# Hybrid decoder step: the third weight tile ahead of the gate sums, two modulation blocks strung through it

## What is computed

```
mod = silu(c) @ w_ada + b_ada -> shift, scale, gate
h   = rms_norm(x) * (1 + scale) + shift
z   = h @ w_in      # att q,k,v,gate | mLSTM q,k | v | o | gate | i,f logits | merge gates A, B
A   = attention: prompt causal over own and past blocks of 256; samples: the 3 best of 8 cached
      blocks of 256 keys by q . mean(k), from a paged cache of 128-row pages, plus themselves
B   = conv(4) + silu on q,k; mLSTM (4 heads, qk 128, v 256) with exponential input gate, sigmoid
      forget gate and running maximum; per-head norm; output gate
u   = sigmoid(ga) * ((A * silu(za)) @ w_att) + sigmoid(gm) * ((B * silu(zm)) @ w_mlstm)
y   = rms_norm(x + gate * (u @ w_out));   also new k, v, C, n, m and conv states
```

## Time and profile before

| | us |
|---|---|
| three runs, median (lowest to highest) | 761.38 (760.47 to 762.78) |
| the profiled execution | 761.64 |
| its span, first to last instruction | 759.9 |
| TensorE busy | 687.3 (90%) |
| TensorE weight loads busy | 617.6 (81%) |
| VectorE busy | 484.9 (64%) |
| GpSimd busy | 467.6 (62%) |
| ScalarE busy | 337.4 (44%) |

### The profile page before, as it was taken

The page is one execution under the profiler, slowest core; times in us unless marked ns, Lnnn a source line. Parts: engine busy times, 40 slices in busy tenths (PEclk is TensorE's granted clock), DMA queues, the critical chain, the costliest instruction groups (busy, mean ns, idle before and its releaser), DMA issues.

```text
span 759.9 us, 14941 instructions
## 1 busy us (share of the span) xinstructions
PE 687.3 (90%) x5066; PEld 617.6 (81%) x5066; DVE 484.9 (64%) x467; ACT 337.4 (44%) x760; POOL 467.6 (62%) x294
## 2 busy tenths in 40 slices
PE   2789999998989789966999999999899999999992
PEld 0565788786868768965999999999799998999992
DVE  1530479998998975867679479498766259333222
ACT  5533483836264335434436446342422224333554
POOL 4210167665676814886698878957495556666652
PEclk9989799999999989997999999999799999999997
DMA  8973868988898871267596588579247355832102
GB/s 318 329 251 128 261 183 239 283 233 273 241 278 263 234 238 28 63 195 209 152 276 202 165 257 245 167 217 268 56 111 221 97 169 154 264 95 83 56 0 113
DMA packets 156903, 144.70 MB, mean 190 GB/s; under 512 B 7547, under 2 KB 115152, under 8 KB 156852
## 3 DMA queue, kind: packets, MB, share of 16 engines
q1 hardware_dynamic: 142696, 136.10, 59.8%
q10 hardware_dynamic: 14164, 8.07, 3.4%
HBM read 135.10 MB, written 9.11 MB: 190 GB/s over the span
## 4 chain that ended last, share of the span: by engine, by line
PE 52%; issue 13%; POOL 12%; DVE 11%; DMA 4%; SPq 4%; ACT 3%; POOLq 0%; ACTq 0%; DVEq 0%
PE ps L539 40%; POOL sb_wL L1408 5%; POOL sb_arenaA L1450 3%; POOL sb_arenaA L1480 3%; DVE sb_arenaA L1866 3%; SPq L391 2%; SPq L392 2%; PE ps L571 1%; PE ps L766 1%; PE ps L805 1%; DVE sb_arenaB L1871 1%; DMA sb_arenaA<-in_w_ada 1%; DMA sb_arenaB<-in_x_sample 1%; PE ps L643 1%; DVE sb_arenaA L1728 1%
## 5 line engine op out<-in xcount | busy, mean ns | idle before, releaser
L1408 POOL TENSOR_TENSOR sb_wL<-sb_wraw,sb_wH 128x512 fp32r<-128x512 f32 (+1 forms) x176 | 232.5, 1338 | 188.7 <-ACT sb_wH L951 173.5
L539 PE MATMUL ps<-sb_hH,sb_wH 128*128 128x260 f32 x1152 | 242.0, 292 | 10.6 <-DVE sb_hL L1632 6.8
L539 PE MATMUL ps<-sb_hL,sb_wH 128*128 128x260 f32 x1152 | 235.6, 287 | 0.0
L539 PE MATMUL ps<-sb_hH,sb_wL 128*128 128x260 f32 x1152 | 235.6, 286 | 0.0
L539 PEld LDWEIGHTS ps<-sb_hH,sb_wH 128*128 128x128 f32 x1152 | 181.8, 193 | 22.4 <-issue 17.0
L951 ACT ACTIVATE sb_wH<-sb_wraw 128x512 fp32r<-128x512 f32 (+1 forms) x176 | 103.5, 612 | 189.3 <-PE ps L539 131.3
L539 PEld LDWEIGHTS ps<-sb_hL,sb_wH 128*128 128x128 f32 x1152 | 181.9, 193 | 0.0
L539 PEld LDWEIGHTS ps<-sb_hH,sb_wL 128*128 128x128 f32 x1152 | 181.3, 192 | 0.0
L1480 POOL TENSOR_TENSOR sb_arenaA<-sb_arenaA 128x2048 f32<-128x2048 f32 x32 | 115.9, 3628 | 8.1 <-DMA sb_arenaA<-in_cache_v 6.1
L1450 POOL TENSOR_TENSOR sb_arenaA<-sb_arenaA 128x2048 f32<-128x2048 f32 x12 | 60.9, 5079 | 30.3 <-DMA sb_arenaA<-in_cache_k 30.3
L1728 DVE TENSOR_REDUCE sb_arenaA<-sb_arenaA 128x2048 f32 (+1 forms) x32 | 72.8, 2285 | 3.3 <-DVE sb_arenaA L1724 2.5
(11 more groups left out here) (356 smaller groups left out, 951.4 us busy)
## 6 DMA issues: line engine op xcount, KB each, us to landing
sb_wraw<-in_w_in SPq DMA_DIRECT2D x64, 512.0 KB, 5.2
sb_arenaA<-in_cache_k SPq DMA_DIRECT2D x128, 256.0 KB, 3.1
sb_arenaA<-in_cache_v SPq DMA_DIRECT2D x128, 256.0 KB, 3.4
sb_arenaA<-in_w_ada SPq DMA_DIRECT2D x6, 2048.0 KB, 12.3
sb_arenaB<-in_state_C SPq DMA_DIRECT2D x8, 512.0 KB, 4.0
sb_wraw<-in_w_mlstm SPq DMA_DIRECT2D x8, 512.0 KB, 4.4
sb_wraw<-in_w_out SPq DMA_DIRECT2D x8, 512.0 KB, 3.9
sb_arenaB<-in_x_prompt SPq DMA_DIRECT2D x1, 2048.0 KB
```

The lines of the kernel that those rows point to most:

```text
L539: last = mm(ps[:, 2 * s + a, 0:HALF], w[:, s, k, :], x[:, k, a * HALF:(a + 1) * HALF], start=(k == 0 and w is wH and x is xH), stop=(k == ...
L1408: tt(wL[:, j % 2, part], wraw[:, j % 4, part], wH[:, j % 2, part].bitcast(F32), ALU.subtract)\
```

## The change

- **Start and pair 0, TensorE.** Block 2 moves ahead of tile 0 (bank 2 instead of 4), block 3 and both turns ahead of tile 1's first half. Half of the gate logits comes before tile 0's second half, the other half strung through it, one k behind each k of the tile (`beside`). Tile 2 moves from behind the first scores to ahead of the gate sums, and blocks 5 and 6 are strung through it: behind k = 0..3 two k of block 5 each, behind k = 4..7 two k of block 6 each (`late_blocks`). The turned gate rows go to bank 7 instead of 6.
- **ScalarE** copies block 2 out before the activations k = 4, 6, takes the convolution states after block 3, and copies blocks 5 and 6 out behind the keys (tile 1).
- **GpSimd** leaves out the product of key step 5 in the last pair; **VectorE** does it itself after the loop. The loop over pairs on GpSimd is one trip shorter, with the last pair written out.
- **VectorE** reduces value pair 4 of head 0 behind the convolutions of head 1 instead of ahead of them.

```
--- before.py
+++ after.py
@@ -35,6 +35,7 @@
 AH, DH = 8, 64
 AW = AH * DH
 PAIRS = AW // P
+LAST = PAIRS - 1
 MH, MQ, MV = 4, 128, 256
 PAGE, PAGES = 128, 16
 NBLK = 8
@@ -524,7 +525,7 @@
             mm = nc.tensor.matmul
             tr = nc.tensor.transpose
 
-            def ztile(j, n, xH, xL, ks=KT, part_ready=None, pages_of=None, parts=(0, 1)):
+            def ztile(j, n, xH, xL, ks=KT, part_ready=None, pages_of=None, parts=(0, 1), beside=None):
                 s = j % 2
                 for half in parts:
                     if half == 0:
@@ -538,6 +539,8 @@
                                 for a in range(2):
                                     last = mm(ps[:, 2 * s + a, 0:HALF], w[:, s, k, :], x[:, k, a * HALF:(a + 1) * HALF],
                                               start=(k == 0 and w is wH and x is xH), stop=(k == ks - 1 and w is wL))
+                        if beside:
+                            beside((k,))
                     if half == 0:
                         last.then_inc(z_half, 1)
                 if pages_of is not None:
@@ -564,13 +567,14 @@
             last.then_inc(t_x, 1)
             pe.wait_ge(c_T, 1)
 
-            def modulation(i, bank):
+            def modulation(i, bank, ks=range(KT)):
                 pe.wait_ge(ld_ada[i % 2], 16 * (i // 2 + 1))
-                for k in range(KT):
+                for k in ks:
                     g = k % 4
                     last = mm(ps[32 * g:32 * g + 32, bank, :], (hS if i == W_Q else cT)[:, k, :], ada[:, i % 2, k, :],
                               start=(k < 4), stop=(k >= 4))
-                last.then_inc(ada_used, 1)
+                if k == KT - 1:
+                    last.then_inc(ada_used, 1)
 
             def mod_turn(count, slot, bank, col):
 
@@ -606,29 +610,31 @@
             prompt_turn(range(4, KT))
 
             pe.wait_ge(v_col, 1)
+            pe.wait_ge(mod_rdy, 2)
+            modulation(2, 2)
             ztile(0, T_ATT, hH, hL, part_ready=h_lo, parts=(0,))
-            pe.wait_ge(xT_act, 3)
-            modulation(2, 4)
-            ztile(1, T_ATT + 1, hH, hL, parts=(0,))
             pe.wait_ge(xT_dve, 5)
+            modulation(3, 5)
             mod_turn(3, 0, 7, 0)
             pe.wait_ge(ld_st, 16)
             pe.wait_ge(xT_act, 4)
             for k in range(KT):
                 last = tr(ps[:, 6, 24 * k:24 * k + 24], stC[:, k * P:(k + 1) * P], ident[0:24, 0:24])
             last.then_inc(t_x, 1)
-            modulation(3, 5)
             mod_turn(4, 1, 7, 36)
-
-            def gate_logits():
-                pe.wait_ge(if_lo, 1)
-                pe.wait_ge(xT_dve, 5)
-                for k in range(KT):
+            ztile(1, T_ATT + 1, hH, hL, parts=(0,))
+
+            def gate_logits(ks):
+                for k in ks:
                     for x in (hH, hL):
                         for bank, cols in ((4, slice(0, T // 2)), (5, slice(T // 2, NT))):
                             last = mm(ps[0:4 * MH, bank, 0:cols.stop - cols.start], wif2[:, k, :], x[:, k, cols],
                                       start=(k == 0 and x is hH), stop=(k == KT - 1 and x is hL))
-                last.then_inc(gt_mm, 1)
+                if k == KT - 1:
+                    last.then_inc(gt_mm, 1)
+
+            pe.wait_ge(if_lo, 1)
+            gate_logits(range(KT // 2))
 
             def qk(e, t):
                 r = slice(DH * e, DH * e + DH)
@@ -669,12 +675,11 @@
                 if before:
                     ztile(0, n, hH, hL)
                 else:
-                    ztile(0, n, hH, hL, part_ready=h_lo, parts=(1,))
+                    ztile(0, n, hH, hL, part_ready=h_lo, parts=(1,), beside=gate_logits)
                 if before:
                     pe.wait_ge(pnorm, 2 * t)
                     ptrans(1)
                 else:
-                    gate_logits()
                     modulation(W_Q, 7)
                 ztile(1, n + 1, hH, hL, parts=(0, 1) if before else (1,))
                 if not before:
@@ -683,16 +688,18 @@
                     pe.wait_ge(st_ev, 1)
                     mm(ps[0:B, 6, :], groupsum[:, 0:B], modp[:, 0, :], start=True, stop=True).then_inc(q_mm, 1)
                     pe.wait_ge(gt_ev, 1)
-                    modulation(5, 5)
                     pe.wait_ge(consts, 3)
-                    pe.wait_ge(q_ev, 1)
                     for j in range(TT + 1):
                         tok = slice(j * P, min((j + 1) * P, NT))
-                        last = mm(ps[0:tok.stop - tok.start, 6, 8 * j:8 * j + 8], gT[:, tok], pairsum[:, :],
+                        last = mm(ps[0:tok.stop - tok.start, 7, 8 * j:8 * j + 8], gT[:, tok], pairsum[:, :],
                                   start=True, stop=True)
                     last.then_inc(g_mm, 1)
-                    modulation(6, 4)
-
+
+                    def late_blocks(ks):
+                        k, = ks
+                        modulation(5 + k // 4, 5 - k // 4, range(2 * (k % 4), 2 * (k % 4) + 2))
+
+                    ztile(2, n + 2, hH, hL, beside=late_blocks)
                     pe.wait_ge(g_dve, 3)
                     for j in range(TT):
                         last = mm(ps[:, 7, MH * j:MH * j + MH], upper[:, :], lf[:, j, :], start=True, stop=(j == 0))
@@ -700,6 +707,7 @@
                             last = mm(ps[:, 7, MH * j:MH * j + MH], ones[:, :], lf[:, i, :], start=False,
                                       stop=(i == j - 1))
                     last.then_inc(g_pe, 1)
+                    pe.wait_ge(q_ev, 1)
                     mod_turn(5, 1, 6, 0)
                     mod_turn(6, 0, 6, 36)
                     pe.wait_ge(q_lo, 1)
@@ -716,8 +724,9 @@
                     for j in range(TT):
                         last = tr(ps[0:MH, 7, j * P:(j + 1) * P], ec[:, j, :], ident[:, :])
                     last.then_inc(g_pe, 1)
-                ztile(2, n + 2, hH, hL)
-                if not before:
+                if before:
+                    ztile(2, n + 2, hH, hL)
+                else:
 
                     pe.wait_ge(g_dve, 5)
                     for j in range(TT):
@@ -1027,14 +1036,14 @@
             high(0, 0, 0)
             high(1, 1, 0)
             prompt_high(0)
+            ada_leave(2, 2, 1).then_inc(ada_ev, 1)
             turned_out(4)
             turned_out(6)
-            ada_leave(2, 4, 1).then_inc(ada_ev, 1)
-            act.wait_ge(t_x, KT + 4)
-            f(stT[:, :, :].rearrange("p k n -> p (k n)"), ps[:, 6, 0:192], ACT.Copy).then_inc(st_ev, 1)
             act.wait_ge(ld_small, 64)
             f(wif2[:, :, 0:2 * MH], wif[:, :, :], ACT.Copy).then_inc(if_hi, 1)
             ada_leave(3, 5, 2).then_inc(ada_ev, 1)
+            act.wait_ge(t_x, KT + 4)
+            f(stT[:, :, :].rearrange("p k n -> p (k n)"), ps[:, 6, 0:192], ACT.Copy).then_inc(st_ev, 1)
             prompt_high(1)
 
             def gate_rows():
@@ -1116,11 +1125,12 @@
                     gate_rows()
                     ada_leave(W_Q, 7, 3).then_inc(qp_ev, 1)
                     sample_queries()
-                    ada_leave(5, 5, 4).then_inc(ada_ev, 1)
                     gate_logs()
-                    ada_leave(6, 4, 4).then_inc(ada_ev, 1)
                 samples_kept(1, n + 1, t)
                 leave(1, n + 1, kT, ACT.Copy)
+                if not before:
+                    ada_leave(5, 5, 4).then_inc(ada_ev, 1)
+                    ada_leave(6, 4, 4).then_inc(ada_ev, 1)
                 copy_out(0, t, before)
                 high(3, n + 3, quad)
                 weights(0, t)
@@ -1450,9 +1460,9 @@
                 tt(four, four, qbc[:, s // 4:s // 4 + 1, :].broadcast_to([P, STEP_PAGES, AW]), ALU.mult)\
                     .then_inc(pool_mult, 1)
 
-            def attention(t, before):
+            def attention(t, first, last):
                 n = T_ATT + 4 * t
-                if not before:
+                if first:
                     low(2, n + 2)
                     query_low()
                     low(3, n + 3)
@@ -1462,11 +1472,13 @@
                 low(2, n + 6)
                 key_step(7, t)
                 low(3, n + 7)
-                key_step(5, t)
-
-            attention(0, False)
-            with pool.Fori(0, PAIRS - 1) as t:
-                attention(t + 1, True)
+                if not last:
+                    key_step(5, t)
+
+            attention(0, True, False)
+            with pool.Fori(0, PAIRS - 2) as t:
+                attention(t + 1, False, False)
+            attention(PAIRS - 1, False, True)
 
             def causal_weights(h):
 
@@ -1657,9 +1669,9 @@
             def gates_in():
                 dve.wait_ge(g_mm, 1)
                 dve.wait_ge(ld_small, 64)
-                tt(G[:, 0:TT, :], ps[:, 6, 0:32].rearrange("p (j n) -> p j n", n=8),
+                tt(G[:, 0:TT, :], ps[:, 7, 0:32].rearrange("p (j n) -> p j n", n=8),
                    bif[:, :].unsqueeze(1).broadcast_to([P, TT, 8]), ALU.add)
```

(15 more changed lines are left out.)

33 lines of the change are left out of this document (17 added, 16 removed).

## The result

The changed kernel is slower, where I had forecast slightly faster. Over all its 20 runs it has a median of 763.85 us (759.49 to 768.55), the kernel before 760.57 us (754.97 to 762.87) in 20 runs beside them. The ratio is 1.005, with a 95% interval of 1.0033 to 1.0068: +3.8 us, between +2.5 and +5.2. The time lies in my range (755.0 to 765.0), the direction was wrong.

A forecast was written before the change was run, and what follows sets the result against it. TensorE was taken as a little over half of the bounding chain, with VectorE's and GpSimd's work the chain in places. The terms +2.1 - 0.8 - 2.6 = -1.3 took 761.38 to 760.1 us; range 755.0 to 765.0.

The forecast's parts named there:

- Head 0 to head 1: Between the heads: earlier convolutions let head 1's tile 1 start earlier, partly lost to low clock; -2.6 us, bounds -5.05 and -1.6.
- the 5.05 us: Head 1's weight tile 1: TensorE starts it at 354.4 instead of 359.45 us, before 2.4 us lost to low clock.
- No gain at head 1's page sums: Sign in the profile after, at head 1, that would show the forecast wrong.
- Pair 0: Start and first pair: holes go, but strung blocks and lost cover delay all behind; +2.1 us, bounds +0.5 and +5.5.
- stringing: Tile 2 in pair 0: eight strung steps cost 9.5 us where two whole blocks cost 4.1.
- the loss of the cover behind the scores: Pair 0 behind the scores: TensorE idles some 4 us without tile 2, then tile 3 loses 2.4 us to low clock.
- Pair 3: Last key steps: GpSimd's last product goes to VectorE, whose products then run unslowed; -0.8 us, bounds -1.6 and +1.0.
- The first: Rival, all three places: holes cost little clock; -6.2 us in sum, 755.2 us; chance 0.26.
- The second: Rival, pair 0: clock falls once more, near 43 us or in the strung tile; +3.8, 765.2 us; chance 0.18.
- The third: Rival, pair 0: strung halves overlap like whole blocks, 5.4 us less; -6.7, 754.7 us; chance 0.06.
- The fourth: Rival, end of pair 3: the edit gives +1.0 in place of -0.8; 761.9 us; chance 0.08.

The follow-up runs named there:

- tile1_only: Kernel before with SP loading weight tile 1 of heads 1 to 3 ahead of value pages 0, value pair 4 unmoved: 761.0 against 759.42 us, ratio 1.0002.
- pair4_only: Kernel before with only head 0's value pair 4 moved behind head 1's convolutions: 763.37 against 761.35 us, ratio 1.0019.
- pair4_tile1: Kernel before with value pair 4 of head 0 moved and weight tile 1 of heads 1 to 3 loaded ahead of value pages 0: 757.45 against 761.35 us.
- pair0_only: Kernel before with only the change's edits of the start and of pair 0: 763.75 against 761.35 us, ratio 1.0046.
- start_only: Kernel before with the new start, but blocks 5 and 6 whole around the gate rows and tile 2 behind the first scores: 754.54 against 760.85 us.
- start_step5_pair4_tile1: Kernel before with start_only's edits, key step 5 and value pair 4 moved, weight tile 1 ahead of value pages 0: 749.63 against 759.42 us.
- pair0_whole: As pair0_only, but block 5 whole ahead of the gate rows and block 6 whole behind tile 2: 759.72 us against 760.85 of the kernel before.
- pair0_fours: As pair0_only, but four k of a block behind every second k of tile 2: 760.79 us against 760.85 of the kernel before.
- after_again: The changed kernel run and profiled once more, on the chip of the last runs: 765.61 us against 759.42 of the kernel before, ratio 1.0093.
- step5_only: Kernel before with only the last pair's key step 5 product moved from GpSimd to VectorE: 759.5 against 761.35 us, ratio 0.9987.
- after: First profile of the changed kernel, all edits against the kernel before; the profiled execution took 759.49 us, its median is 763.85 us.

## Why the prediction was wrong

**Head 0 to head 1: the step that failed.** I forecast -2.6 us there; alone this edit measured +1.4. I wrote that ScalarE converts the tile, empties the other and copies, "in that order, and TensorE starts tile 1 at 354.4 instead of 359.45". The queue, the load and ScalarE's order were right: counted from the start of head 0's gated output (326.48 in the trace before, 321.51 after), the forecast has the load land at 25.0, and it landed at 24.9. The instruction that waits for it was wrong. `z_free` counts the PSUM slots that have been emptied. TensorE waits for it at n + 6 ahead of the first value transposes, and tile 0 stands behind them in its order:

```
pe.wait_ge(z_free, n + 6)
for u in range(2):
    ...                                       # four value transposes
    if not first:
        ztile(u, n + 4 + u, hH, hL, ...)      # u = 0 is tile 0
```

The count n + 6 comes from the copy behind weight tile 1's conversion. I had let tile 0 pass and only tile 1 wait. At 27.9 us behind the start of the gated output, where the forecast starts tile 1, it is tile 0 that starts; tile 1 starts at 36.0, and at 33.0 before. So none of the 5.05 us was there to gain. In the trace before, the scores end at 352.15 (347.52 + 4.63) and the transposes begin behind the load's chain:

```profile
352.58 0.66 PE L784 MATMUL ps<-sb_ident,sb_arenaB 128*128 128x128 f32 x4 [0.42 <-ACT sb_vS L958]
```

The load's chain was already the later of the two, by 0.4 us; in the six profiles with neither edit it is 0.1 to 1.3. The edit brought forward only the scores. The load landed at 24.2 before and lands at 24.9, 0.7 later because the convolutions now stand ahead of the value pair that frees the pages' buffer. Tile 0 started at 26.8 and starts at 27.9. And it starts behind 15.29 us of idling, where the scores ran just ahead of it before: it takes 7.66 us, the first 4.5 at half clock, against 5.77. Together that is +3.0 in the profiles.

Over all fourteen profiles, the time from the start of that output to the start of head 1's page sums is 37.4 to 39.1 us in the seven without the edit (tile1_only among them), 41.6 to 41.9 in the three with it alone, and 32.9 to 34.9 in the four with it and the SP order. No gain at head 1's page sums was what I had named as a sign of being wrong. The timing of pair4_only gives +1.4, with an interval that leaves out my bounds of -5.05 and -1.6. That the load is the wait is shown by pair4_tile1 against pair4_only; that the two were level before is shown by the trace before, and agrees with tile1_only, which gains nothing.

**Pair 0: the mechanism right, the size low.** Forecast +2.1 with bounds +0.5 and +5.5; measured +3.5 (+1.8 to +5.3). The places agree: modulation 2 and half of tile 0 end at 39.4 (forecast 39.2), the strung tile takes 15.2 us (15.2), the scores start at 80.8 (81.5), the hole behind them is 3.79 us (some 4), tile 3 ends at 98.9 (100.2). What was off, as far as the profiles show, is the base. The one trace before was slow there: its second scores' maximum starts at 102.7, and in the five other profiles with the old pair 0 between 100.2 and 102.5, 101.5 in the mean of all six. In the four with the new pair 0 the mean is 104.6. That difference is +3.1; mine was against the slowest of six.

What its steps are worth, from the timings (each difference within some 3 us, pair0_only measured on another chip than the rest, each against the kernel before on its own): the start of the edit -6.5, tile 2 moved ahead of the scores +5.1 (with ScalarE's later copies), stringing +4.9 (forecast: 5.4). The same steps read from the profiles, at the start of the second scores' maximum (start_only 96.9 and start_step5_pair4_tile1 97.1, pair0_whole 99.2, pair0_only and its like 104.6, pair0_fours 100.6), are -4.4, +2.2, +5.4, and 4.0 back for filled columns, where the timings have 2.9. I had the loss of the cover behind the scores as a small item, a low clock of 2.4 us. Both ways tile 2 ahead of the scores loses: it leaves TensorE without work during VectorE's chain, and that costs more than the wait for block 6 that it hides. How much more, 2 or 5 us, isn't settled; single profiles of one kernel shift by as much. Of stringing, pair0_fours gives a part back, by filled columns and half as many changes. The Trainium skill ("TensorEngine Tiling (Array Packing)", Key Properties) says that column tiles work independently; x4 in 1.05 us against x8 in 1.07 agrees.

**Pair 3: the size borne out, the mechanism in part.** Forecast -0.8, measured -1.0 (-3.0 to +1.0). In the profile after, the two products took 2.38 and 2.40 us instead of the 6.60 of one. But the slow product of 6.60 behind the loop stands in the one trace before only. In the seven other profiles in which GpSimd has step 5, VectorE's product behind the loop takes 2.5 us, and the slow one (5.7 to 6.6) is the product before it, the last in the loop, beside GpSimd's product of step 7. That one the edit doesn't touch, and it is still there in three of the six profiles with the edit, as in after_again (VectorE, then GpSimd):

```profile
242.63 6.18 DVE L1736 TENSOR_TENSOR sb_arenaA<-sb_arenaA 128x2048 f32<-128x2048 f32 x1
...
242.08 4.58 POOL L1460 TENSOR_TENSOR sb_arenaA<-sb_arenaA 128x2048 f32<-128x2048 f32 x1 [4.05 <-DMA sb_arenaA<-in_cache_k]
```

In all fourteen profiles one of these two engines' products is slow: VectorE's takes 5.7 to 6.7 us where GpSimd's began first (ten), GpSimd's 6.4 to 6.8 where VectorE's began first or level (four, the trace before and the one after among them). From the start of VectorE's last product in the loop to the copy behind the key sums (sb_selfp) the eight profiles without the edit take 21.1 to 23.2 us, the six with it 18.5 to 22.6; the means differ by 2.5. So the sign, a gain, rests on the traces; the timing alone holds no change too.

**Rivals.** The first, that holes cost little clock, is refuted: every long hole is followed by 0.50 here too, and its -5.05 wasn't there. The second is refuted in its mechanism (1.00 through the whole strung tile); that its +3.8 is the measured difference is luck. The third is refuted by the 15.2 us. The fourth, +1.0 in pair 3, stands at the edge of step5_only's interval, and the traces speak against it. What happened was none of them: that the edit between the heads could lose was no case of mine, since both bounds of that term were gains. Of the 5.1 us between forecast and result some 4.0 lie in that term and 1.4 in pair 0.

## What to carry to other kernels

When an edit takes one wait away, list every wait of the next instruction on that engine with its time of release; the gain is what lies between it and the latest of the others; here another was already the later, by 0.4 us.

Work that fills another engine's chain is worth what it covers: move it only if what it leaves behind is covered again.

And take the base of a forecast from more than one execution where the clock or a load's landing can shift the stretch by more than the change is worth.

## What of the hardware was unexpected

- The clock stayed at full speed through 15.2 us of alternating 128-column and half-filled 32-column matmuls (granted clock 1.00, busy 15.20 of 15.20).
- The first head's scores in pair 0, on half of the rows and behind small products, ran at half clock to their end in each of the fourteen profiles (4.63 us), though nothing interrupts them. The second head's, on half of the rows too but soon after tile 3, took 2.42 us for a third more columns. Head 1's scores, on all rows, took 2.32 us behind a row of tiles and 4.05 to 4.63 behind a wait of 11.5 to 12.0 us.
- Of two products of 128x2048 that met on VectorE and GpSimd at the end of pair 3, one kept its own time (2.28 or 4.6 us) and the other took 5.7 to 6.8. Which one changed between two executions of the same kernel: GpSimd's 6.76 in after, VectorE's 6.18 in after_again.
- One kernel's executions spread over 9 us (759.49 to 768.55) on one core, against 3.8 for the whole change.
